# Second FFN matrix by one level of Strassen over eight of nine token tiles

## The reference

```python
a, b = jnp.split(h @ w_ffn_in_l, 2, axis=-1)
x = x + gate2 * rms_norm((jax.nn.silu(a) * b) @ w_ffn_out_l, norm_g_l[3])
```

## Time and profile before

| | us |
|---|---|
| median of 3 runs | 1831.42 (1829.01 to 1832.5) |
| profiled execution, its own time | 1835.74 |
| its span in the profile | 1833.9 |
| TensorE busy | 1764.9 (96%) |
| VectorE busy | 798.0 (44%) |
| ScalarE busy | 619.4 (34%) |
| mean granted TensorE clock | 0.984 of 2.4 GHz |

### The profile page before, as it was taken

The page is one execution under the profiler, slowest core; times in us unless marked ns, Lnnn a source line. Parts: engine busy times, 40 slices in busy tenths (PEclk is TensorE's granted clock), DMA queues, the critical chain, the costliest instruction groups (busy, mean ns, idle before and its releaser), DMA issues.

```text
span 1833.9 us, 24582 instructions
## 1 busy us (share of the span) xinstructions
PE 1764.9 (96%) x9754; PEld 1637.7 (89%) x9754; DVE 798.0 (44%) x1256; ACT 619.4 (34%) x1064; POOL 404.7 (22%) x476
## 2 busy tenths in 40 slices
PE   6999999999999999999999899999999999999997
PEld 3899998979999999987878799999999999888885
DVE  4400012333334444345867874444444433454543
ACT  6311123232222222223656572222222223343432
POOL 0400001322122233342414352222222210000000
PEclk9999999999999999999999999999999999999998
DMA  9544445654355566687857232222222226667572
GB/s 352 200 168 159 170 142 189 222 180 134 127 180 177 177 197 198 207 238 222 265 174 236 94 116 73 72 73 72 72 72 72 73 73 195 205 183 228 177 235 74
DMA packets 175880, 296.84 MB, mean 162 GB/s; under 512 B 12201, under 2 KB 122348, under 8 KB 175770
## 3 DMA queue, kind: packets, MB, share of 16 engines
q1 hardware_dynamic: 131904, 163.80, 27.8%
q0 software_dynamic: 27536, 91.31, 15.2%
q10 hardware_dynamic: 16336, 40.29, 6.6%
HBM read 227.58 MB, written 67.82 MB: 161 GB/s over the span
## 4 chain that ended last, share of the span: by engine, by line
PE 82%; DVE 5%; DMA 4%; POOL 2%; issue 2%; ACT 2%; SPq 1%; ACTq 0%; DVEq 0%; POOLq 0%
PE bank L545 25%; PE bank L547 25%; PE bank L546 25%; DMA mg<-z_scratch 1%; PE bank L757 1%; PE bank L1002 1%; PE bank L1005 1%; DVE w_lo L1716 1%; PE bank L1012 1%; PE bank L1020 1%; DMA ada_raw<-in_w_ada 1%; SPq L640 1%; DVE mg L2040 1%; DMA zt<-z_scratch 1%; POOL ya L2466 1%
## 5 line engine op out<-in xcount | busy, mean ns | idle before, releaser
L1716 DVE TENSOR_TENSOR w_lo<-raw,w_hi 128x1024 fp32r<-128x1024 f32 x218 | 281.6, 1294 | 387.1 <-ACT w_hi L1255 386.8
L545 PE MATMUL bank<-h_hi,w_hi 128*128 128x384 f32 x1080 | 377.4, 349 | 8.1 <-DVE h_lo L2247 5.4
L546 PE MATMUL bank<-h_lo,w_hi 128*128 128x384 f32 x1080 | 367.4, 340 | 0.0
L547 PE MATMUL bank<-h_hi,w_lo 128*128 128x384 f32 x1080 | 367.1, 340 | 0.0
L1255 ACT CAST w_hi<-raw 128x1024 fp32r<-128x1024 f32 x218 | 226.2, 1049 | 295.2 <-PE bank L547 174.0
L545 PEld LDWEIGHTS bank<-h_hi,w_hi 128*128 128x128 f32 x1080 | 205.5, 190 | 25.4 <-ACT z_st L1314 10.1
L546 PEld LDWEIGHTS bank<-h_lo,w_hi 128*128 128x128 f32 x1080 | 205.3, 190 | 0.1
L547 PEld LDWEIGHTS bank<-h_hi,w_lo 128*128 128x128 f32 x1080 | 205.1, 190 | 0.0
L547 PE MATMUL bank<-w_hi,f_lo 128*128 128x512 f32 x396 | 158.0, 399 | 0.0
L546 PE MATMUL bank<-w_lo,f_hi 128*128 128x512 f32 x396 | 156.0, 394 | 0.0
L545 PE MATMUL bank<-w_hi,f_hi 128*128 128x512 f32 x396 | 155.2, 392 | 0.0
(11 more groups left out here) (318 smaller groups left out, 3157.9 us busy)
## 6 DMA issues: line engine op xcount, KB each, us to landing
raw<-in_w_stream SPq DMA_DIRECT2D x208, 512.0 KB, 4.4
z_scratch<-z_st ACTq DMA_DIRECT2D x44, 576.0 KB, 3.1
raw<-in_w_ada SPq DMA_DIRECT2D x35, 512.0 KB, 5.7
mg<-z_scratch ACTq DMA_DIRECT2D x24, 576.0 KB, 6.6
f_raw<-f_scratch SPq DMA_DIRECT2D x66, 192.0 KB, 4.3
zt<-z_scratch POOLq DMA_DIRECT2D x27, 256.0 KB, 3.7
xp_scratch<-x_in POOLq DMA_DIRECT2D x9, 512.0 KB, 12.6
raw<-in_k_dft SPq DMA_DIRECT2D x9, 512.0 KB, 3.5
```

Of the source, the lines that this page charges most:

```text
L545: pe.matmul(out, a_hi, b_hi, start=start, stop=False)
L546: pe.matmul(out, a_hi, b_lo, start=False, stop=False)
L547: return pe.matmul(out, a_lo, b_hi, start=False, stop=stop)
L1716: dve.tensor_tensor(w_lo[:, slot], raw[:, slot], w_hi[:, slot].bitcast(F32), ALU.subtract).then_inc(s_wlo, 1)
```

## The change

`fo` is rewritten. f is taken as 2 x 2 blocks (rows of k: 11 and 11 tiles; tokens: tiles 0 to 3 and 5 to 8), the weights as 2 x 2 blocks (11 k tiles each, 512 columns each). Seven products of blocks (order 1, 7, 5, 6, 4, 2, 3) replace eight. Token tile 4 (`ALONE`) stays out and is multiplied plainly beside products 1, 7, 2 and 3, into banks 6 and 7. There are 77 steps: one k of one product, of 12 matmuls, or 15 where tile 4 takes part.

- Loads: f is stored with all tokens in one row. A step loads 512 or 640 columns of f, in products 7 and 5 another 512 into `a_aux` (3 buffers), and one half row of weights (256 KB, four pieces of 512 bytes per partition), in 7 and 5 two. f has 8 slots, the weights 8 half slots.
- Sums: `a_sum` (f) in products 7, 5, 6, 3, and `b_sum` (weights) in 7, 5, 6, 4, one operation of 512 columns each per step, all on VectorE, chained over the products in `S_ch` and `T_ch`.
- Splits: `fo_high` on ScalarE, `fo_low` on VectorE; in product 7 a second weight half for tile 4.
- Evacuation: products use 4 of 6 ring banks. ScalarE copies products 1, 7 and 5 to `R1`, `R2` (`fo_copy`); VectorE adds products 6, 4, 2, 3 (`fo_sum`, `fo_rest`, `fo_c21`, `fo_c11`, `fo_c12`). Both come three steps after a product's last step in the engine's list.
- Order of the output tiles: 5, 6, 7, 8, 4, 0, 1, 2, 3. The last product does its last 6 k tiles tile by tile, 4 first.

The core of the diff ("..." marks what is left out, removed lines among it):

```diff
+FO_ORDER = (1, 7, 5, 6, 4, 2, 3)
+FO_ALONE = (1, 7, 2, 3)
+FO_ASUM, FO_BSUM, FO_TWO = (7, 5, 6, 3), (7, 5, 6, 4), (7, 5)
+FO_B = {1: ((0, 0),), 7: ((1, 1), (0, 1)), 5: ((0, 1), (0, 0)), 6: ((0, 0),), 4: ((1, 0),), 2: ((1, 0),), 3: ((1, 1),)}
+FO_A = {1: ((0, 0),), 7: ((0, 0), (0, 1)), 5: ((0, 1), (1, 1)), 6: ((0, 0),), 4: ((1, 1),), 2: ((1, 0),), 3: ((1, 0),)}
+KF = FT // 2
+FO_STEPS = KF * len(FO_ORDER)
+AR, AX_R = 8, 3
+ALONE = 4
+FO_TILES = (5, 6, 7, 8, ALONE, 0, 1, 2, 3)
+X1_AT = (30, 31, 32, 65, 67, 70)
+FO_EVAC, FO_FIRST = 3, 4
+SQUARE_AT, OUT_AT = (59, 60, 61, 63), (60, 61, 62, 64)
...
-    f_dram = nc.dram_tensor("f_scratch", (FT, NG, P, GW), F32).ap()
+    f_dram = nc.dram_tensor("f_scratch", (FT, P, T), F32).ap()
...
+        def fo_operand(s):
+
+            return s + fo_count(s, (7,))
...
+        def operand_free(eng, o):
+
+            if o < 2 * RAW:
+                unit_done(eng, U_FO - RAW + o // 2)
+            else:
+                step_done(eng, max(s for s in range(FO_STEPS) if fo_operand(s) <= o - 2 * RAW))
...
+                if e < 2 * RAW:
+                    sp.wait_ge(s_whi, split_index(U_FO - RAW + e // 2) + 1)
+                    sp.wait_ge(s_wlo, split_index(U_FO - RAW + e // 2) + 1)
                 else:
...
+                    b = next(v for v in range(FO_STEPS) if fo_load(v, len(FO_B[fo_product(v)]) - 1) >= e - 2 * RAW)
+                    if fo_product(b) in FO_BSUM:
+                        b_sum_done(sp, b)
+                    second = e - 2 * RAW - fo_load(b, 0)
+                    if fo_product(b) not in (6, 4) and (fo_product(b), second) not in ((7, 0), (5, 1)):
+                        sp.wait_ge(s_whi, split_index(U_FO) + fo_operand(b) + second + 1)
+                        sp.wait_ge(s_wlo, split_index(U_FO) + fo_operand(b) + second + 1)
...
+            def a_load(s):
+                i, k = fo_product(s), s % KF
+                rows, cols = FO_A[i][0]
+                if s == 0:
+                    sp.wait_ge(s_prod, product_done(PAIRS - 1, 4))
+                    for g in range(2):
+                        sp.wait_ge(s_fs[g], 16 * PAIRS)
+                elif s >= AR:
+                    step_done(sp, s - AR)
+                c0 = 640 * cols
+                sp.dma_start(a_raw[:, s % AR, 0:a_width(s)], f_dram[KF * rows + k, :, c0:c0 + a_width(s)]).then_inc(s_al[s % AR], 16)
+                if i in FO_TWO:
+                    x = fo_count(s, FO_TWO)
+                    if x == 0:
+                        sp.wait_ge(s_fs[2], 16 * PAIRS)
+                    if x >= AX_R:
+                        a_sum_done(sp, next(v for v in range(FO_STEPS) if fo_product(v) in FO_TWO and fo_count(v, FO_TWO) == x - AX_R))
+                    rows, cols = FO_A[i][1]
+                    sp.dma_start(a_aux[:, x % AX_R], f_dram[KF * rows + k, :, 640 * cols:640 * cols + 512]).then_inc(s_axl[x % AX_R], 16)
...
+            for s in range(FO_STEPS):
+                a_load(s)
+                for x in range(len(FO_B[fo_product(s)])):
+                    b_load(s, x)
+                if s in X1_AT:
+                    x1_load(X1_AT.index(s))
+            for r in range(len(X1_AT), NT):
+                x1_load(r)
...
+            def fo(p):
+                i = FO_ORDER[p]
+                tail = KF - (6 if p == len(FO_ORDER) - 1 else 3)
+
+                def ready(s):
+                    pe.wait_ge(s_flo, s + 1)
+                    pe.wait_ge(s_wlo, split_index(U_FO) + fo_operand(s) + (2 if i == 7 else 1))
+
+                def piece(k, t):
+                    s = KF * p + k
+                    o = fo_operand(s)
+                    if t < 4:
+                        bh, bl = fo_weights(o)
+                        return mm3(pe, fo_bank(p, t)[:, :], a_hi[:, s % AR, ktile(t)], a_lo[:, s % AR, ktile(t)], bh, bl,
+                                   k == 0, k == KF - 1)
+                    bh, bl = fo_weights(o + 1 if i == 7 else o)
+                    return mm3(pe, bank[6 if i in (1, 2) else 7][:, :], a_hi[:, s % AR, ktile(4)], a_lo[:, s % AR, ktile(4)],
+                               bh, bl, k == 0 and i in (1, 7), k == KF - 1 and i in (2, 3))
+
+                def bank_free(t):
+                    if p == 0:
+                        if t == 0:
+                            pe.wait_ge(s_pv, OV)
+                        elif t == 4:
                             pe.wait_ge(s_fp, PAIRS)
...
+                    elif t < 4:
+                        b, u = divmod(4 * p + t - 6, 4)
+                        if b < 0:
+                            return
+                        if FO_ORDER[b] in (1, 7, 5):
+                            pe.wait_ge(s_pact, OS + 4 * b + u + 1)
+                        else:
+                            pe.wait_ge(s_pv, {6: V_SUM, 4: V_C21, 2: V_C11}[FO_ORDER[b]] + u + 1)
+
+                for k in range(tail):
+                    ready(KF * p + k)
+                    for t in fo_tiles(p):
+                        if k == 0:
+                            bank_free(t)
+                        m = piece(k, t)
                     m.then_inc(s_unit, 1)
...
+                for t in fo_tiles(p):
+                    end = t == fo_tiles(p)[-1]
+                    for k in range(tail, KF):
+                        if t == fo_tiles(p)[0]:
+                            ready(KF * p + k)
+                        m = piece(k, t)
+                        if end and k < KF - 1:
                             m.then_inc(s_unit, 1)
...
+                    m.then_inc(s_unit if end else s_ot, 1)
...
+            def fo_high(s):
+                i, o, a = fo_product(s), fo_operand(s), s % AR
+                if i in FO_ASUM:
+                    a_sum_done(act, s)
                 else:
...
+                    a_landed(act, s)
+                w = a_width(s)
+                act.copy(a_hi[:, a, 0:w], S_ch[:, s % KF] if i in (5, 6) else a_raw[:, a, 0:w]).then_inc(s_fh, 1)
+                if i in FO_BSUM:
+                    b_sum_done(act, s)
+                else:
+                    fo_landed(act, fo_load(s, 0))
+                operand_free(act, o)
+                act.copy(fo_weights(o)[0], T_ch[:, s % KF] if i in (7, 6, 4) else fo_raw(fo_load(s, 0))).then_inc(s_whi, 1)
+                if i == 7:
+                    operand_free(act, o + 1)
+                    act.copy(fo_weights(o + 1)[0], fo_raw(fo_load(s, 1))).then_inc(s_whi, 1)
+
+            def fo_copy(p, t):
+                tile_done(act, p, t)
+                act.copy((R1[:, t, 0], R2[:, t, 1], R1[:, t, 1])[p], fo_bank(p, t)[:, :]).then_inc(s_pact, 1)
...
+            def fo():
+                for s in range(FO_FIRST, FO_STEPS):
+                    fo_high(s)
+                    p, k = divmod(s - FO_EVAC, KF)
+                    if k == KF - 1 and p < 3:
+                        for t in range(4):
+                            fo_copy(p, t)
+                    if s in SQUARE_AT:
+                        o_square(SQUARE_AT.index(s))
+                for r in range(len(SQUARE_AT), NT):
+                    o_square(r)
...
+                out, left, right, op = {7: (a, a, a_aux[:, x], ALU.subtract), 5: (ch, a, a_aux[:, x], ALU.add),
+                                        6: (ch, ch, a, ALU.subtract), 3: (a, a, ch, ALU.subtract)}[i]
+                dve.tensor_tensor(out, left, right, op).then_inc(s_tw, 1)
...
+                out, a, b, op = {7: (ch, left, right, ALU.subtract), 5: (left, left, right, ALU.subtract),
+                                 6: (ch, ch, left, ALU.add), 4: (ch, ch, left, ALU.subtract)}[i]
+                dve.tensor_tensor(out, a, b, op).then_inc(s_S, 1)
...
+            def fo_low(s):
+                i, o, a, w = fo_product(s), fo_operand(s), s % AR, a_width(s)
+                dve.wait_ge(s_fh, s + 1)
+                dve.tensor_tensor(a_lo[:, a, 0:w], S_ch[:, s % KF] if i in (5, 6) else a_raw[:, a, 0:w],
+                                  a_hi[:, a, 0:w].bitcast(F32), ALU.subtract).then_inc(s_flo, 1)
...
+            def fo_sum(t):
+                tile_done(dve, FO_ORDER.index(6), t)
+                dve.wait_ge(s_pact, OS + 12)
+                dve.tensor_tensor(R2[:, t, 0], R1[:, t, 0], fo_bank(3, t)[:, :], ALU.add).then_inc(s_pv, 1)
+
+            def fo_rest(t):
+                dve.wait_ge(s_pv, V_SUM + t + 1)
+                dve.tensor_tensor(R1[:, t, 1], R1[:, t, 1], R2[:, t, 0], ALU.add).then_inc(s_pv, 1)
+                dve.tensor_tensor(R2[:, t, 0], R2[:, t, 0], R2[:, t, 1], ALU.add).then_inc(s_pv, 1)
+                dve.wait_ge(s_pv, V_REST + 3 * t + 1)
+                dve.tensor_tensor(R2[:, t, 1], R2[:, t, 1], R1[:, t, 1], ALU.add).then_inc(s_pv, 1)
+
+            def fo_c21(t):
+                tile_done(dve, FO_ORDER.index(4), t)
+                dve.wait_ge(s_pv, V_REST + 3 * t + 2)
+                dve.tensor_tensor(R2[:, t, 0], R2[:, t, 0], fo_bank(4, t)[:, :], ALU.subtract).then_inc(s_pv, 1)
...
```

(67 more changed lines are left out.)

300 lines of the change are left out of this document (143 added, 157 removed).

## The result

The changed kernel takes 1811.05 us (median of 4 runs, 1808.61 to 1813.64) against 1830.74 for the kernel before: ratio 0.9893, 95% interval 0.9878 to 0.9909, so 19.7 us faster. Two later sets of runs of the same kernel gave 1808.49 against 1831.69 (ratio 0.9878, 0.9860 to 0.9896) and 1811.55 against 1830.34 (0.9889, 0.9870 to 0.9909). The forecast was 25.9 us faster, at 1805.5, with a range that held the time.

The account below looks back on a forecast made before the run. The prediction took TensorE's number of matmuls, plus what follows the last one, to bound the stage. Matmuls -30.8, loads +1.8 and tail +3.1 gave -25.9 us, so 1805.5 us on the median, range 1801 to 1817.

Parts of the forecast that it names:

- Matmuls: TensorE in the second FFN matrix's stage: 1056 matmuls instead of 1188, 132 fewer at 0.2333 us each, -30.8 us.
- rival (e): TensorE: matmul distance isn't 0.2333 us when operands change every third matmul; 10 ns more costs 10.6 us, 1816; chance 0.02.
- VectorE: Sums and low parts, priced at 0.607 us per queued 512-column operation, stay hidden behind TensorE: cost 0, margin 1.7 us.
- Product 4: Extra sums take 12.1 us on VectorE where 10.8 are free; the lead covers the overrun: cost 0.
- The banks: Evacuation of product results: ScalarE's copies free the banks in time, cost 0, cover 1.6 us.
- the start of the stage: Preparing the first four steps takes 5.4 us within the 8.3 us of the preceding matmul pair: cost 0.
- Rival (c): VectorE binds at full durations plus hand-over (0.73 us) in products 7, 5, 6, 4: +8 us, 1812 to 1814; chance 0.12.
- Loads: DMA falls behind in product 5; step 32 is late in its tail: +1.8 us once, bounds 0 and +6.
- rival (b): Loads bind over products 7 and 5 at 298 or 270 GB/s: 6 to 15 us unhidden, 1810 to 1819; chance 0.17.
- rival (a): All loads hidden and the tail after the last matmul shorter, 0.7 to 3.1 us: 1801.3 to 1803.7; chance 0.15.
- The rule of the Trainium skill: About 358 GB/s of HBM per core binds the loads; step 32 would land some 2.5 us later.
- After the last matmul: Output tiles take 4.95 us each in series against TensorE's 4.2: end at +7.3 instead of +4.3, cost +3.1 us.

Follow-up runs that it names:

- the run with both edits: Changed kernel with VectorE's low parts of a step ahead of the next step's sums, and first three x1 tiles loaded behind steps 44, 46, 48: 1805.17 us.
- The run with the exchanged order: Changed kernel with VectorE doing the low parts of step s before, not behind, the sums of step s + 1: 1804.55 us.
- first repeat: The changed kernel run again without edits, in a later set: 1808.49 us.
- x1 later: Changed kernel with the first three x1 tiles loaded behind steps 44, 46 and 48 instead of 30, 31 and 32: 1807.46 us.

## Why the prediction was right and where it was off

**Matmuls, right.** The 132 removed ones were worth 30.8 us: with no wait left (the run with both edits) the stage is 276.8 - 246.0 = 30.8 shorter. The distance stayed at 0.2333: in that run the first of the 1056 matmuls starts at 1541.07 and the last at 1787.24, 246.17 us for 1055 distances. So rival (e) is out.

**VectorE, right.** A queued operation of 512 columns starts 0.60 us after the one before, as priced from the earlier trace rows. Product 4, which overran its steps on paper, cost TensorE nothing. The banks and the start of the stage cost nothing either. Rival (c), which used full durations and a hand-over, 0.73, is out: the distance is 0.60, product 7 lost nothing, and from step 27 on VectorE waits for transfers in every step of product 5.

**Loads, right place, wrong size.** The forecast put TensorE's only stall into the tail of product 5, on a step whose weights land last: that is where it is. Its rates held; two of the three medians, 1811.05 and 1811.55, lie in rival (b)'s 1810 to 1819, but by another way than (b)'s 270 to 298 GB/s. A step of product 5 takes 3.15 to 3.23 us of transfer (forecast 3.24), an x1 tile 1.25 (1.31), and the stretch runs at 338 GB/s. Step 32's sum of weights starts at 1640.97, which is 62.3 us after the start of product 7 (1578.71; forecast landing 61.1). And yet 1.8 us became 7.0, by two steps that the working left out:

1. "From landing to ready are sum of f, sum of weights, ScalarE's copy and the last low part", all of one step. I had read the order of VectorE's list, `a_sum(s + 1)`, `b_sum(s + 1)`, `fo_low(s)`, and used it for the load on the engine, but not for its waits. Each low part stands behind a wait for the next step's weights. So not only step 32 was late but step 31 too (ready at 1642.87, wanted at 1640.3), and step 32 stood behind both sums of product 6's first step. That made 3.7 to 4.3 us of waiting out of 1.8. The run with the exchanged order has 1.7: the number of the forecast, in the kernel that the forecast had in mind. That it is so close is in part luck. There the sum of weights of step 32 starts 62.0 us after the start of product 7 (at 1578.27), 0.9 later than the forecast's landing, and its low part ends 2.1 us behind that start instead of the forecast's 3, because the sum of f was already done when the weights landed:

```profile
1640.26 0.69 DVE L2373 TENSOR_TENSOR raw<-raw 128x512 f32<-128x512 f32 x1 [1.07 <-DMA raw<-in_w_stream]
...
1641.63 0.69 DVE L2382 TENSOR_TENSOR w_lo<-raw,w_hi 128x512 fp32r<-128x512 f32 x1
```

2. No price for the clock. The earlier trace rows show 1.00 over the stage, and the sum took 0.2333 for every matmul. Behind 4.3 us of idling, broken by three matmuls, 11 came at the lower level: 2.2 us. In the runs with 1.7 to 2.5 us of waiting the loss beyond the waits was 0.2 to 0.5, in those with 3.7 to 4.3 it was 2.0 to 2.8.

The bounds of this term were off too. The working says that at 340 GB/s for all loads step 32 lands at 57 and costs 0. By its own chain, in which step 27 is issued at 37.1 with 2 us to the first byte, six steps and two x1 tiles at 340 GB/s end at 60.7, and the cost is 1.4. A cost of 0, as in rival (a), needs some 363 GB/s by the same chain.

The rule of the Trainium skill that was weighed (DMA: Bandwidth & Descriptors, Where 436 GB/s comes from: some 358 GB/s of HBM per core) does not bind this core. 412, 403 and 388 GB/s in the earlier trace rows are above it, and so is an x1 tile in 1.25 us, which is 419 GB/s. The steps' loads ran at 330 to 345 GB/s at full share, between the mix of before and the rows of 4 KB in the earlier trace rows. The 2.5 us that the prediction took from that page were too much even by its own chain: six steps and two x1 tiles with 0.524 MB of long rows each come to 1.2 us more at 358 than at 400, an estimate from the page's figure. Step 32 did land 1.2 us later than my sum, but the lateness was there before those steps: step 27's sum of weights starts 43.8 us after the start of product 7 (at 1622.55), where the forecast had its landing at 42.3.

**After the last matmul, right mechanism, wrong bound.** The serial chain is as forecast: 4.9 us a tile, and VectorE ends 7.5 us after the last matmul's start, 2.8 more than before (forecast 3.1). But the span's end doesn't hang on VectorE's, it hangs on POOL's last store, issued 0.75 us after the last matmul in before and 2.9 in after: +2.1, and the span's end moved by +2.2. The prediction equated the two ends, and the earlier trace rows held no POOL line to correct it with. It cost only 0.9 us in the sum, since both moved alike, but it hid 4.4 us that lay open in the changed kernel and 5.1 in the one before.

**The sum.** By the stage -30.8 + 7.0 + 2.2 = -21.6 us, and by the three pairs of medians -18.8 to -23.2, against -25.9 foreseen. The difference of 4.3 between stage and forecast is 5.2 of the load term less 0.9 of the tail. That the spans of the two profiles differ by 26.0, the forecast to 0.1, is chance: 4.4 of it lie ahead of the stage.

## What to carry to other kernels

Where an engine works ahead in order, look at each wait in its list and ask what finished work is queued behind it: prepare step s completely before waiting for step s + 1. Count the tail of a product as an early need: "tile by tile" both asks for its last steps sooner and reports their buffers free later, and here a tail of one step instead of three was worth 3.4 to 4.0 us in product 7 and 5.3 to 5.9 in product 5. And ask of the very end which queue's last transfer sets it, before you shorten the chain in front of it.

## What the runs showed of the hardware

- The span ends 11.5 to 11.6 us after POOL's last transfer is issued, in all ten traces in which POOL stores the last tile but one, although that store lands after some 2.9 us. With the last two stores on SP's queue the end came 2.5 us after VectorE's last addition, in the kernel before as in the changed one. What POOL or its queue does in between no trace shows.
- TensorE's granted clock can halve in mid-kernel behind a short stall: 2.54 us idle, three matmuls, 1.73 us idle, and then 11 distances of 0.43 us on average instead of 0.2333. In another trace of the same kernel (first repeat) it was at the lower level right behind the first wait, of 2.48 us:

```profile
1641.66 0.76 PE L658 MATMUL bank<-w_hi,a_hi 128*128 128x512 f32 x1 [2.48 <-DVE w_lo L2382]
1642.22 0.63 PE L659 MATMUL bank<-w_lo,a_hi 128*128 128x512 f32 x1
```

  A single wait of 1.74 us left it at 1.00, and so did waits of 0.69 and 1.84 us with three matmuls between them.
- The time of the same work ahead of the stage, 1535.5 to 1544.8 us, moves more than most of the edits here. Of the medians alone, the one of "x1 later" would have told 1.0 us for an edit that is worth 4.0 in the stage of its trace.
